# Branch products cut into rounded parts and dealt among the attention pairs of a one-core transformer kernel

## What is computed

```python
h = _rms(x, norm1_g)
(a_q, a_k, a_v, i_q, i_k, i_w, b_q, b_kv, b_g, c_qkv, mix_g) = _split_last(h @ w_in, IN_SIZES)
y_a = dsa_attention(...) @ w_branch_a     # 8 heads over the top 64 keys of an index score; 512 columns
y_b = nsa_attention(...) @ w_branch_b     # 8 heads, each the gated sum of a compressed, a selected and a
                                          # window softmax; gates sigmoid(b_g); 512 columns
y_c = dilated_attention(...) @ w_branch_c # 4 heads, each over three dilation groups; 256 columns
g = sigmoid(mix_g).reshape(bsz, seq, 3, D_MODEL)
x = x + (g[:, :, 0] * y_a + g[:, :, 1] * y_b + g[:, :, 2] * y_c) @ w_out
h = _rms(x, norm2_g)                      # then a gated feed-forward layer
```

## Time and profile before

| | us |
|---|---|
| Median of 3 runs | 1243.98 (1242.55 to 1248.61) |
| The profiled execution | 1247.74 |
| Its span, first to last instruction | 1245.9 |
| Mean granted TensorE clock | 0.956 of full |

### The profile page before, as it was taken

How to read it: one execution, slowest core, us unless ns; L and a number is a source line. 1 busy time by engine, 2 the same in 40 slices (tenths; PEclk the granted TensorE clock), 3 DMA queues, 4 the chain that set the end, 5 groups by cost and what they waited for, 6 DMA issues and landing times.

```text
span 1245.9 us, 16919 instructions
## 1 busy us (share of the span) xinstructions
PE 1135.7 (91%) x6975; PEld 967.5 (78%) x6975; DVE 787.5 (63%) x1027; ACT 485.8 (39%) x630; POOL 99.7 (8%) x84
## 2 busy tenths in 40 slices
PE   4878999879999997799999699987999988999998
PEld 2665886769999775799988598875766547999977
DVE  2386858678778788785544757467767355455443
ACT  2242434434333332333333446453665334433332
POOL 0000000000000000000000001062445100000000
PEclk9888999889999999799999899997999998999999
DMA  9694561657987984279556345551224344565462
GB/s 342 253 383 155 203 230 50 238 193 238 324 281 276 344 295 145 90 219 295 179 169 202 111 156 169 169 169 34 94 77 133 100 139 136 171 193 179 149 223 102
DMA packets 145950, 236.97 MB, mean 190 GB/s; under 512 B 4949, under 2 KB 86354, under 8 KB 145746
## 3 DMA queue, kind: packets, MB, share of 16 engines
q1 hardware_dynamic: 138944, 221.12, 52.5%
q10 hardware_dynamic: 6930, 14.77, 3.2%
HBM read 229.32 MB, written 6.55 MB: 189 GB/s over the span
## 4 chain that ended last, share of the span: by engine, by line
PE 74%; DVE 15%; ACT 5%; issue 4%; ACTq 1%; DMA 0%; POOL 0%; DVEq 0%; POOLq 0%
PE bank L564 72%; DVE ring_lo L1549 2%; PE bank L627 2%; ACT w_hi L1163 1%; DVE small L2320 1%; DVE aux L2340 1%; ACT aux L1471 1%; DVE y_tok L1860 1%; DVE small L1862 1%; DVE y_tok L1858 1%; DVE small L2322 1%; DVE aux L2298 1%; ACT y_tok L1471 1%; PE bank L675 1%; ACTq L1195 1%
## 5 line engine op out<-in xcount | busy, mean ns | idle before, releaser
L1549 DVE TENSOR_TENSOR ring_lo<-ring,w_hi 128x2048 fp32r<-128x2048 f32 (+3 forms) x142 | 314.3, 2214 | 294.8 <-ACT w_hi L1163 291.9
L1163 ACT ACTIVATE w_hi<-ring 128x2048 fp32r<-128x2048 f32 (+3 forms) x154 | 285.6, 1857 | 459.2 <-PE bank L564 430.6
L564 PE MATMUL bank<-h_hi,w_hi 128*128 128x256 f32 x1056 | 302.6, 287 | 3.0 <-DVE h_lo L1568 2.8
L564 PE MATMUL bank<-h_lo,w_hi 128*128 128x256 f32 x1056 | 300.4, 284 | 0.0
L564 PE MATMUL bank<-h_hi,ring_lo 128*128 128x256 f32 x1056 | 300.2, 284 | 0.0
L564 PEld LDWEIGHTS bank<-h_hi,w_hi 128*128 128x128 f32 x1056 | 204.3, 193 | 5.3 <-issue 4.6
L564 PEld LDWEIGHTS bank<-h_lo,w_hi 128*128 128x128 f32 x1056 | 204.3, 194 | 1.0 <-issue 1.0
L564 PEld LDWEIGHTS bank<-h_hi,ring_lo 128*128 128x128 f32 x1056 | 204.3, 193 | 0.0
L564 PE MATMUL bank<-w_hi,h_hi 128*128 128x512 f32 (+4 forms) x320 | 128.8, 402 | 19.8 <-DVE h_lo L1796 7.8
L564 PE MATMUL bank<-ring_lo,h_hi 128*128 128x512 f32 (+4 forms) x320 | 124.7, 390 | 0.0
L564 PE MATMUL bank<-w_hi,h_lo 128*128 128x512 f32 (+4 forms) x320 | 124.7, 390 | 0.0
(11 more groups left out here) (259 smaller groups left out, 1445.7 us busy)
## 6 DMA issues: line engine op xcount, KB each, us to landing
aux<-in_w_mod SPq DMA_DIRECT2D x24, 2048.0 KB, 10.3
ring<-in_ffn_w_in SPq DMA_DIRECT2D x88, 512.0 KB, 5.0
ring<-in_w_in SPq DMA_DIRECT2D x24, 1024.0 KB, 4.9
ring<-in_w_ffn_in SPq DMA_DIRECT2D x44, 512.0 KB, 4.7
ring<-in_ffn_w_out SPq DMA_DIRECT2D x20, 1024.0 KB, 5.3
ring<-in_attn_w_qkv SPq DMA_DIRECT2D x12, 1024.0 KB, 13.4
ring<-in_w_ffn_out SPq DMA_DIRECT2D x10, 1024.0 KB, 5.1
bias_rows<-srow ACTq DMA_DIRECT2D x1, 5376.0 KB
```

The lines of the kernel that those rows point to most:

```text
L564: return nc.tensor.matmul(o, l, r, start=start, stop=stop, **kw)
L1163: nc.scalar.activation(panel_part(i, 0), raw_panel(i), ACT.Copy).then_inc(w_hi, 1)
L1549: V.tensor_tensor(panel_part(i, 1), raw_panel(i), panel_part(i, 0).bitcast(F32), ALU.subtract)\
```

## The change

- The branch weights are split into hi and lo like the gates' (hi by ACT, lo by POOL), and the attention outputs too: ACT's `pair_out` writes half of the bank, rounded, into `ft_round`, and a new `pair_low` on DVE writes the rest and frees the bank.
- The list `DENSE` puts the 24 gate pieces and 12 branch pieces in one order. `DENSE_AT` deals 16 to units 1 to 11 and 14 to units 12 to 19; 6 follow behind the last unit. The C branch has two chunks in a piece, the others four.
- Units go in the order B, C, A. The scores of units 0 and 1 are issued behind input blocks 8 and 9, the last two; the C keys' transposes (22, 24, 26) move into units 0 to 2, and all 16 rounds of `top_keys` into units 0 to 7 (before, 4 ran on DVE in each of blocks 8 and 9).
- Gates are made by tanh: sigmoid(v) is (tanh(v/2) + 1)/2; half is already in the branch outputs, and DVE's `gated` forms (gate + 1) times branch result, and adds.
- Stage 1 takes for `z` the four banks that held chunks 0 to 3 of `z_h`.

```diff
-WHOLE = ("pool", "cmp", "branch0", "branch1", "branch2")
+WHOLE = ("pool", "cmp")
+DENSE = [("mix", 0, 1), ("mix", 1, 1), ("mix", 0, 2), ("mix", 1, 2), ("branch", 0, 1), ("branch", 1, 1),
+         ("mix", 0, 0), ("branch", 0, 2), ("branch", 1, 2), ("mix", 1, 0), ("branch", 0, 0), ("branch", 1, 0)]
...
-        lo_by_pool = [key[0] == "mix" for key, *_ in panels]
+        lo_by_pool = [key[0] in ("mix", "branch") for key, *_ in panels]
...
-        UNITS2 = [(kind, qt, pr) for kind in "CBA" for qt in range(TT) for pr in range(PAIRS[kind])]
+        UNITS2 = [(kind, qt, pr) for kind in "BCA" for qt in range(TT) for pr in range(PAIRS[kind])]
...
+        N_EARLY, N_LATE = 16, 14
+        DENSE_AT = {u: [] for u in range(len(UNITS2))}
+        for i in range(N_EARLY):
+            DENSE_AT[1 + i * 11 // N_EARLY].append(pieces[i])
+        for i in range(N_LATE):
+            DENSE_AT[12 + i * 8 // N_LATE].append(pieces[N_EARLY + i])
+        DENSE_END = pieces[N_EARLY + N_LATE:]
...
@@ TensorE
                 if nb == 8:
                     z_emptied(7)
                     features(0, 2)
+                    for b0 in (12, 14):
+                        wait_emptied(pe, ("ft", b0))
+                    scores2(0, "side")
                 if nb == 9:
-                    pe.wait_ge(k_normed, 2)
-                    features(22, 24, 26)
+                    scores2(1, "side")
                     pe.wait_ge(cmp_p_done, 1)
                     transposes("cmpT", [cmp_probs[:, qt, :] for qt in range(TT)], "side")
+            POOLS["z"] = tuple(where[("z_h", ch)][0] for ch in range(4))
+            POOLS["side"] = tuple(where[("z_h", ch)][0] for ch in range(4, 8))
...
             for u in range(len(UNITS2)):
                 turn_probs2(u)
...
+                    scores2(u + AHEAD, unit_pool(u + AHEAD))
+                if u < 3:
+                    features(22 + 2 * u, pool="unit")
+                for piece in DENSE_AT[u]:
+                    dense_piece(piece, "mix" if u < 12 else "mixA")
...
                 values2(u)
-            for nb in range(2):
-                for br in range(3):
-                    n = 2 if br == 2 else 4
-                    gemm(f"branch{br}", lambda tt, c: token_tile([ft], 8 * br + c, tt), range(TT), nb, NB,
-                         [(0, n)])
+            for piece in DENSE_END:
+                dense_piece(piece, "mixA")
@@ ACT
+            def next_high(piece):
+                kind, nb, br, kg, tt = piece
+                if tt == TT - 1:
+                    split_to(panel_at[(kind, (nb, br), kg)] + PARTS)
...
+                    nc.scalar.activation(dst, src, ACT.Copy, scale=0.5).then_inc(pair_hi, 1)
...
+                for piece in DENSE_AT[u - 1] if u else ():
+                    next_high(piece)
                 if u + AHEAD < len(UNITS2):
                     exps2(u + AHEAD)
...
             pair_out(len(UNITS2) - 1)
+            for piece in DENSE_AT[len(UNITS2) - 1]:
+                next_high(piece)
+            for piece in DENSE_END:
+                mix_out(piece)
+                next_high(piece)
             highs("mixed", hT[0], ACT.Copy)
@@ DVE
             for u in range(len(UNITS2)):
                 if u + 1 < len(UNITS2):
                     weigh(u + 1)
                 if u + AHEAD < len(UNITS2):
                     logits(u + AHEAD)
+                if u:
+                    pair_low(u - 1)
+                    for piece in DENSE_AT[u - 1]:
+                        gated(piece)
...
+            for piece in DENSE_END[:-1]:
+                gated(piece)
+            split_to(first_out)
+            gated(DENSE_END[-1])
```

More of the change, by code:

```diff
@@ L964, in _, with dense_piece, scores2 @@
             mix_w = {}
-            def mix_piece(i):
-                b, kg, tt = i // 4, i % 4 // 2, i % 2
+            def dense_piece(piece, pool):
+                kind, nb, br, kg, tt = piece
+                key = (kind, (nb, br))
                 if tt == 0:
-                    mix_w[kg] = panel(("mix", b, kg))
+                    mix_w[kg] = panel(key + (kg,))
                 if kg == 0:
[L972 to L978, removed]
+                    take(key + (tt,), pool)
+                bank = psum[where[key + (tt,)][0]]
+                chunks = 2 if (kind, br) == ("branch", 2) else PK
+                last = kind == "branch" or kg == 1
+                for c in range(chunks):
+                    if kind == "mix":
+                        own = token_tile(hT, kg * PK + c, tt)
+                    else:
+                        if c == 0:
+                            wait_emptied(pe, ("O2", 2 if br == 2 else {0: 3, 1: 0}[br] + tt))
+                        own = out_tile(br, c, tt)
+                    ins = product(bank[:, :], own, [x[:, c, :] for x in mix_w[kg]],
+                                  kg == 0 and c == 0, last and c == chunks - 1)
+                if last:
+                    fills(ins, key + (tt,))
                 if tt == TT - 1:
-                    release(("mix", b, kg), ins, ("mix", b, tt) if kg == 1 else None)
-            def scores2(u):
+                    release(key + (kg,), ins, key + (tt,) if last else None)
+            def scores2(u, pool):
                 kind, qt, pr = UNITS2[u]
@@ L986, in scores2 @@
                 segs = pair_segments(kind, pr)
-                banks = [take(("S2", u, i), "unit") for i in range(4 if kind == "C" else 2)]
+                banks = [take(("S2", u, i), pool) for i in range(4 if kind == "C" else 2)]
                 order = [(half, s) for s in range(len(segs)) for half in range(2)]
@@ L1128, in _, with unit_pool @@
                 beside(nb)
[L1129 to L1133, removed]
+            def unit_pool(u):
+                return "unitA" if UNITS2[u][0] == "A" else "unit"
             for u in range(len(UNITS2)):
@@ L1451, in _ @@
+                    split_to(last_panel("z", len(Z_BLOCKS) - 1) + 1)
+            split_to(last_panel("z", len(Z_BLOCKS) - 1) + 2)
+            exps2(1)
             empties(nc.scalar.activation(pcT, v3(result(act, "cmpT")[:, 0:TT * P], TT), ACT.Copy), "cmpT")
[L1453 to L1460, removed]
@@ L1463, in exps2 @@
[L1463 to L1467, removed]
-                n, width = (4, nk) if kind == "B" else (2, SEGS[kind] * nk)
-                for i in range(n):
-                    part = lbuf[u % 3][:, i * width:(i + 1) * width]
-                    ins = nc.scalar.activation(part, part, ACT.Exp, bias=small[:, o + i:o + i + 1],
-                                               accum_out=small[:, o + 4 + i:o + 5 + i])
-                ins.then_inc(exp2_done, 1)
@@ L1488, in _ @@
-            for u in range(AHEAD):
-                exps2(u)
             for u, (kind, qt, pr) in enumerate(UNITS2):
@@ L2421, in mix_lo @@
                     wait_hi(pool, i)
-                    for c in range(PK):
+                    for c in range(panels[i][2]):
                         ins = nc.gpsimd.tensor_tensor(panel_part(i, 1)[:, c, :], raw_panel(i)[:, c, :],
```

257 lines of the change are left out of this document (147 added, 110 removed).

## The result

The changed kernel takes 1255.08 us, median of 9 runs (1248.37 to 1256.97). The kernel before takes 1243.98 in the 9 runs beside it (1240.79 to 1249.16). The ratio of the means is 1.0071, 95% interval 1.0045 to 1.0097 (the medians alone would give 1.0089); in a later series it was 1.0066 (1.0044 to 1.0088). The forecast was no change, 1244. So it is 0.7% slower: a small loss, beyond the 0.5% that I had called the limit of what can be told. The median stands at the very upper end of the range, 1255, so the number is held by the width of the range and not by its middle.

The account below looks back on a forecast made before the run. TensorE was taken to bound the units and branches, with waits at head and tail removable. Gains and losses summed to +0.4 on the profiled 1247.74, so 1248.1, carried to the median as 1244; range 1233 to 1255.

Parts of the forecast that it names:

- Head of the units: Before the first turned blocks: earlier scores cut TensorE's wait, ACT's queue is late next; a gain of 6.5 net, 7.7 less 1.2.
- rival (b): B and C units: DVE becomes the bound, its products slowed beside POOL; 12 us more, 1256; chance 0.21.
- first turned block before 841: Sign at the head of the units: the first turned block comes before 841, the second near 845.
- Start of stage 1: Stage 1 may start sooner with the banks of chunks 0 to 3; a gain of 2.4, between 1.6 and 3.2.
- Branch products: Branch stage: three matmuls on rounded parts replace two fp32 passes, 27.3 for 40 chunks; a gain of 8.6.
- Panel waits: Units 17 to 19 and behind: panels split too late, waits of 2.5, 6.4, 4.5 and 2.3; a loss of 15.7.
- Rival (a): Last units: panels are ready anyway, so the waits fall; 1234 if half goes, 1225 if all; chance 0.31.
- Bank 7: Units 4 and 8: the bank is freed later, by `pair_low` behind `weigh` and `logits`; a loss of 2.5, bounds 0 and 6.
- Tail: From the last branch matmul to `w_out`: the chain is kept, 6.8 for 7.2; a gain of 0.4.
- Ordinary waits and clock: In the units, ordinary waits gain 3.1, bounds 0 and 10; two clock falls behind new waits lose 3.2, bounds 0 and 6.
- Rival (c): Units: tanh outside exp's table brings two loads per readout, 31 on ACT, half showing; 1260; chance 0.03.

Follow-up runs that it names:

- experiment 1: Changed kernel, with POOL not starting the first two gate panels' low parts until unit 1's weights are done on DVE: 1255.7 us, ratio 1.0075 to the kernel before.
- experiments 2: Changed kernel, with DVE instead of POOL making the low parts of four late panels: 1242.83 us, ratio 0.9964 to the kernel before.
- experiment 3: Changed kernel, with ACT making the next panel's hi part directly behind the readout, not a unit later: 1248.60 us, ratio 1.0005 to the kernel before.
- experiment 10: Changed kernel, with sigmoid in place of tanh in the readout of the mixing gates, which alters the gates' values: 1265.41 us, one run.
- experiments 5: Changed kernel plus experiments 2, 3 and 4, POOL's wait of experiment 1, and DVE making the first gate panel's low part: 1238.33 us, ratio 0.9930 to the kernel before.
- experiment 7: Experiment 5's kernel, with early hi parts only from unit 16 and without experiment 4's edit: 1231.16 us, ratio 0.9863 to the kernel before.
- experiment 8: Experiment 7's kernel, with ACT's second gate panel hi part behind unit 1's exponentials and the compressed probabilities' copy: 1230.23 us, ratio 0.9865 to the kernel before.
- experiment 4: Changed kernel, with DVE making a full output bank's low part before the next logits, not behind them: 1250.04 us, one run.

## Why the prediction was right or wrong, step by step

The forecast of the stretch was 314.7 + 0.4 = 315.1; it measures 322.5, 7.4 more. Its mechanism held for the branch products, the panels and bank 7, and failed at the head of the units.

**Head of the units: the step that failed.** The gain here was put at 7.7 with ACT's queue as the last to be ready. I said that what is late next is ACT, with unit 1 turned at 845.2, less the 2.4 of an early start: 842.8. It was turned at 849.76. ACT ended its queue at 841.8, sooner than the 843.6 that I gave it. DVE was late. `weigh(0)` and `weigh(1)` each cost 0.9 by themselves; beside POOL they cost 4.91 and 1.84, with 1.1 for the tiny product before each. I had that very mechanism, and its row, in rival (b), where I asked it of the B and C units. I had never laid POOL's eight subtractions, which the change puts directly behind two hi parts, over the DVE work at the head. The experiment that lets POOL wait removes 5.7 of the 8.47. In the stretch's time my forecast for unit 1's turned block, with only 0.1 of the early start, as in this trace, is 842.8 - 707.3 + 2.3 = 137.8; the changed kernel has it at 143.3, experiment 1 at 137.4, or 139.0 with the dip that it was spared. So ACT's queue was about right, and POOL beside DVE is some 4.3 of the 5.5. The Trainium skill (SBUF — State Buffer, "SBUF: two separate sides") calls the port pair of VectorE and GpSimd an exclusive lock that is held for a whole instruction. The rows agree, 1.23 for 1.23. They also agree with its list of who takes the lock: beside POOL in experiment 1, a reduction of 128x512 took 0.69 (839.14) and the two logits from PSUM 0.88 (838.16), as without POOL. The other 1.2 of the 5.5 may be TensorE's clock, 4.7 us at 0.50 behind T0; I had counted 2.5 for unit 0. No run separates it. The forecast "first turned block before 841" is what failed first.

**Start of stage 1.** Expected 2.4; by the traces without a dip it is 1.7, inside my bounds of 1.6 and 3.2, because TensorE meets the second block's panel 1.79 late, as I had named. The profiled execution shows only 0.1, for it has the dip of 1.6, a term that my sum didn't have. Whether an earlier start makes a dip likelier stays open: of the ten traces with the new banks six have one in stage 1, of the two with the old banks none.

**Branch products.** Right. The last two pieces run as one stream, with matmuls at 1016.53 and 1021.66 as the second and last of 24 (some records between them are missing), 0.233 apart (forecast 0.227), in three forms, so 40 chunks cost 28.0 for 27.3.

```profile
1016.53 0.39 PE L606 MATMUL bank<-ring_lo,features_round 128*128 128x512 f32 x1
...
1021.66 0.39 PE L606 MATMUL bank<-w_hi,features_round 128*128 128x512 f32 x1
```

**Panel waits.** Right: four where they were forecast, 2.49, 6.33, 4.26 and 3.00 for 2.5, 6.4, 4.5 and 2.3, 16.1 for 15.7, and experiments 2 and 3 show two of the links that make them. Rival (a), panels ready anyway, is out. **Bank 7.** 1.20 and 2.23, 3.4 for the 2.5 taken; in the bounds. (Two sums of the prediction are slightly off: its parts for bank 7, 1.2 and 1.9, make 3.1 and not 3.5, and 1.3, 1.91 and 5.05 make 8.3 and not 8.4.) **Tail.** The way to `w_out` is 7.1 (1021.90 to 1028.98) for 6.8. **Ordinary waits and clock.** From unit 1's turned block to `w_out` all of it together took 179.2, and by the forecast's own times it is 1022.4 - 842.8 = 179.6. That this agrees to 0.4 is partly luck: panels, bank 7, branch products and tail together came out 2.3 dearer than forecast (0.4, 0.9, 0.7 and 0.3), so the ordinary waits and the clock came out 2.7 cheaper. From 845.04 to 995.50 TensorE is idle 15.4, of which the named waits are 12.3; the other waits are 3.1, where before they were 7.8. The miss of 7.4 on the stretch is thus 2.3 from stage 1 (0.7 of the start, 1.6 of the dip) and 5.5 at the head, less 0.4.

**Rival (b)**, DVE as the bound of the B and C units: no. None of TensorE's waits in those units ended on `weigh`. It was the right mechanism with the wrong address, so my chance of 0.24 for slower was too small. **Rival (c)**: no. There is one table load, at 819.06, before the units and none in them. The Trainium skill (ScalarE: Activation LUTs, "Table sets: the hidden batching unit") has tanh in exp's set, and the trace agrees; experiment 10 is the other side of that rule.

**What stays open**: how much of the gain in experiments 5, 7 and 8 belongs to the head. By the trace it is 5.6 at T0 in experiment 7, less what is given back (4.0 of it in experiment 1); no kernel changed the head alone in a way that the timing could tell.

## What to carry to other kernels

When a change moves work of one engine, lay its whole list of instructions over the timelines of every engine that shares a resource with it, for each place where it now falls, and above all where the pipeline is empty and each instruction is on the path. Ten microseconds of POOL beside DVE's products cost TensorE 5.7 at the head; in the full units no wait of TensorE ended on the products, and with POOL put off to unit 2, in experiment 1, 4.0 of what T0 had gained was lost again in other waits. Taking the clash away from one place is not yet a gain. A panel that is split just in time needs its longest link on the fastest free engine once the cover runs out: 11.5 us here. And an edit that is good for the last units may be bad for the first ones; applied from unit 16 on, the early hi parts, with the low parts of the output banks left where they were, took away the waits of 3.8 and 4.6 that the edit everywhere had brought.

## What the runs showed of the hardware

The granted clock can dip where nothing in the program that I can see differs. Behind the same wait of 1.79 in stage 1, and with the same program up to there, the changed kernel had a granted clock of 0.74 for 6 us, and experiment 8 had 1.00; experiment 7 had a dip of 0.83 over 10 us elsewhere in stage 1, with TensorE busy throughout. Each costs 1.6 by T0 (138.5 against 136.9 in experiment 4, 132.9 against 131.3 in experiments 7 and 8), which is more than some edits are worth. The cause stays open.

```profile
724.88:730.88 6.00, 4.58 (x18) 4.61 (x19) 3.58 (x6) 2.72 (x5) 0.70 (x1) 0.74 0.42 139
```

```profile
726.64:732.64 6.00, 4.59 (x26) 4.62 (x27) 3.57 (x6) 2.84 (x6) 0.70 (x1) 1.00 0.42 139
```

```profile
814.44:824.44 10.00, 10.00 (x63) 8.23 (x61) 7.86 (x13) 6.48 (x9) 10.00 (x7) 0.83 0.20 55
```

Executions of one kernel also lie some 8 us apart: of the 12 of experiment 3, three took 1241.0 to 1241.8 and eight 1248.2 to 1250.3. Edits under 3 us can so be read only in the trace, from one mark to another, and only with the clock of both stretches beside them.
